# Hybrid encoder on one core: value halves stacked in one weight tile, key projections in another PSUM bank, four orders changed

## The reference, cut to what matters

```python
for l in range(2):                       # DEPTH = 2, 512 tokens, 1024 features
    h = rmsnorm(x, norm_mix_g[l])
    proj = h @ w_in[l]                   # latents for q (256), kv (128), k_pe (32), gate (1024)
    o_mla = mla_mixer(...)               # 8 heads; q = latent @ w_uq, [k | v] = latent @ w_ukv
    o_sg = spatial_gating_mixer(...)     # u * (W_s LayerNorm(v) + b), 4 chunks of 128 tokens, 8 groups
    x = x + concat([rmsnorm(o_mla), rmsnorm(o_sg)]) @ w_out[l]
    x = x + memory_attention(...)
    x = x + conv_ffn(...)
```

## Time and profile before

| what | value |
|---|---|
| median of 3 runs | 1485.91 us (1484.67 to 1487.13) |
| the profiled execution, its own time | 1485.62 us |
| its span | 1483.8 us |
| PE busy (matmuls) | 1455.2 us, 98% of the span |
| DVE / ACT / POOL busy | 734.9 / 698.3 / 683.9 us, 50 / 47 / 46% |
| mean granted TensorE clock | 0.996 of full speed |

### The profile page before, as it was taken

One profiled execution on the slowest core, in us unless ns is written; L12 is line 12 of the kernel. 1 busy time (PEld: TensorE's weight loads), 2 busy tenths in 40 slices (PEclk: granted clock), 3 DMA queues, 4 the chain that ended last, 5 costly groups with the idle time before them and its releaser, 6 DMA issues.

```text
span 1483.8 us, 19468 instructions
## 1 busy us (share of the span) xinstructions
PE 1455.2 (98%) x6872; PEld 1198.1 (81%) x6872; DVE 734.9 (50%) x1123; ACT 698.3 (47%) x1134; POOL 683.9 (46%) x343
## 2 busy tenths in 40 slices
PE   9999999999999999999999999999999999999997
PEld 7777789888888888888877777988888888888885
DVE  7738679353455410545264676771535544024533
ACT  6577656353344422444355885553534444224432
POOL 2445348534443454354445543684344354435351
PEclk9999999999999999999999999999999999999998
DMA  5320225412233333232323112463032332323231
GB/s 194 113 83 15 72 90 168 140 44 72 74 104 92 113 100 99 86 108 78 119 82 100 57 29 86 128 185 99 16 99 60 111 113 86 112 86 101 72 97 57
DMA packets 38889, 138.76 MB, mean 94 GB/s; under 512 B 4448, under 2 KB 4704, under 8 KB 38560
## 3 DMA queue, kind: packets, MB, share of 16 engines
q1 hardware_dynamic: 37296, 133.20, 29.2%
q10 hardware_dynamic: 1520, 4.56, 0.9%
HBM read 135.64 MB, written 2.10 MB: 93 GB/s over the span
## 4 chain that ended last, share of the span: by engine, by line
PE 78%; issue 9%; DVE 4%; POOL 4%; ACT 4%; DMA 0%; SPq 0%; POOLq 0%; DVEq 0%; ACTq 0%
PE ps L1461 25%; PE ps L1463 25%; PE ps L1462 25%; POOL w_lo L374 4%; PE ps L1619 1%; ACT work L660 1%; POOL work L442 1%; DVE small L1157 0%; DVE arena L1183 0%; DMA raw<-blocks_d 0%; DVE arena L1319 0%; ACT arena L668 0%; DVE work L1006 0%; ACT arena L633 0%; PE ps L1471 0%
## 5 line engine op out<-in xcount | busy, mean ns | idle before, releaser
L374 POOL TENSOR_TENSOR w_lo<-raw,w_hi 128x1024 fp32r<-128x1024 f32 x244 | 594.2, 2453 | 662.8 <-ACT w_hi L509 662.8
L509 ACT ACTIVATE w_hi<-raw 128x1024 fp32r<-128x1024 f32 x247 | 255.0, 1054 | 329.6 <-PE ps L1463 326.6
L1461 PE MATMUL ps<-h_hi,w_hi 128*128 128x512 f32 (+1 forms) x1040 | 406.8, 391 | 3.2 <-DVE w_lo L972 1.8
L1463 PE MATMUL ps<-h_hi,w_lo 128*128 128x512 f32 (+1 forms) x1040 | 403.7, 388 | 0.0
L1462 PE MATMUL ps<-h_lo,w_hi 128*128 128x512 f32 (+1 forms) x1040 | 403.6, 388 | 0.0
L1461 PE MATMUL ps<-arena,w_hi 128*128 128x512 f32 (+1 forms) x648 | 240.8, 372 | 0.0
L1463 PE MATMUL ps<-arena,w_lo 128*128 128x512 f32 (+1 forms) x648 | 238.8, 369 | 0.0
L1462 PE MATMUL ps<-arena,w_hi 128*128 128x512 f32 (+1 forms) x648 | 238.6, 368 | 0.0
L1461 PEld LDWEIGHTS ps<-h_hi,w_hi 128*128 128x128 f32 x1040 | 195.6, 188 | 46.8 <-issue 3.1
L1462 PEld LDWEIGHTS ps<-h_lo,w_hi 128*128 128x128 f32 x1040 | 195.7, 188 | 40.7 <-issue 1.0
L1463 PEld LDWEIGHTS ps<-h_hi,w_lo 128*128 128x128 f32 x1040 | 195.6, 188 | 40.6
(11 more groups left out here) (200 smaller groups left out, 1815.4 us busy)
## 6 DMA issues: line engine op xcount, KB each, us to landing
raw<-blocks_d SPq DMA_DIRECT2D x247, 512.0 KB, 3.5
work<-memT_d ACTq DMA_DIRECT2D x2, 1024.0 KB, 5.0
x<-xT_d SPq DMA_DIRECT2D x3, 512.0 KB, 7.5
work<-ln_d ACTq DMA_DIRECT2D x2, 512.0 KB, 3.7
outT_d<-work SPq DMA_DIRECT2D x4, 256.0 KB, 2.5
outT_d<-work ACTq DMA_DIRECT2D x4, 256.0 KB, 2.7
x<-xT_d SPq DMA_DIRECT2D x2, 256.0 KB, 4.6
raw<-blocks_d SPq DMA_DIRECT2D x2, 256.0 KB, 4.9
```

The lines of the kernel that those rows point to most:

```text
L374: gp.tensor_tensor(w_lo[:, b % SPLIT, :], raw[:, b % RAW, :], w_hi[:, b % SPLIT, :].bitcast(F32), ALU.subtract).then_inc(lo_done.sem, 1)
L509: act.activation(w_hi[:, b % SPLIT, :], raw[:, r, :], ACT.Copy).then_inc(hi_done.sem, 1)
L1461: pe.matmul(out, a_hi, b_hi, start=first, stop=False)
L1463: return pe.matmul(out, a_lo, b_hi, start=False, stop=last)
```

## The change

```diff
-NORM_STEPS = {(1, 2): 2, (2, 1): 3}
+CENTRED_STEPS = {(1, 1): 2, (1, 2): 3}
+NORM_STEP0 = (1, 2)
+NORM_STEPS = {(1, 3): 2, (2, 1): 3}
-SPLIT_STEPS = ((1, 3), (2, 3), (2, 3), (3, 0))
+SPLIT_STEPS = ((2, 0), (2, 3), (2, 3), (3, 0))
-MIX_STEPS = ((3, 2), (3, 3), (4, 2), (4, 3))
-GATED_STEPS = ((5, 0), (5, 2), (5, 2), (5, 3))
+MIX_STEPS = ((3, 2), (4, 1), (4, 3), (5, 1))
+GATED_STEPS = ((5, 2), (5, 2), (5, 3), (5, 3))
...
+        v_pair = arena[:, 8:16, :]...rearrange("p k (h s d) -> p k h s d", s=2, d=VD)
+        v_hi, v_lo = v_pair[:, :, :, 0, :], v_pair[:, :, :, 1, :]
...
         def k_bank(p):
-            return 5 if p == 0 else 2
+            return 5 if p == 0 else 4
+        def mix_bank(n):
+            return (4, 2)[n % 2]
... ACT
+                act.preload_act_table_set("gelu_apprx_tanh_and_others")   # ahead of the v_hi copies
...
-                def copy_sums(h):
-                    need(spread, h + 1)
+                def copy_part(h):
+                    need(pv_mm, h + 1)
                     if h > 0:
                         need(o_done, h)
-                    act.activation(rsum, ps[sum_bank(h)][0:64, :], ACT.Copy)
+                    act.activation(part, ps[B_PV][64:128, :], ACT.Copy)
+                    if t == 3 and h >= 1:
+                        copy_part(h - 1)
                     turned_hi(i)
-                    if t == 0 and h >= 1:
-                        copy_sums(h - 1)
-                    if t == 0 and h + 2 < HEADS:
+                    if t == h % 2 and h + 2 < HEADS:
                         q_part(h + 2)
-                    if h == HEADS - 1:
-                        gate_turned(t)
+                    if h == HEADS - 1 and t >= 1:
+                        gate_turned(t - 1)
... DVE
                 def attended(h):
-                    need(rsum_done, h + 1)
-                    need(pv_mm, h + 1)
-                    dve.tensor_tensor(o_mla[...], ps[B_PV][0:64, :], rsum, ALU.mult)
+                    need(part_done, h + 1)
+                    dve.tensor_tensor(part, ps[B_PV][0:64, :], part, ALU.add)
+                    need(whole_done, h + 1)
+                    need(spread, h + 1)
+                    dve.tensor_tensor(o_mla[...], ps[sum_bank(h)][0:64, :], part, ALU.mult)
-                    if t == 0 and h + 2 < HEADS:
+                    if t == h % 2 and h + 2 < HEADS:
                         q_part(h + 2)
+                    turned_lo(i)
                     if t == 3 and h >= 1:
                         attended(h - 1)
-                    turned_lo(i)
... PE
                 def q_proj(h):
                     if h >= 2:
                         need(qf_done, h)
+                        if h % 2 == 1:
+                            need(kl_done, h // 2 + 1); need(kst_done, h // 2 + 1)
+                        if h >= HEADS - 2:
+                            need(gated, 4 * (h - HEADS + 2) + 2)
                 def k_proj(p):
-                    if p > 1:
-                        need(rsum_done, 2 * p - 2)
+                    if p > 0:
+                        need(qf_done, 2 * p + 1)
                 def attend(h, ks):
                     for k in ks:
-                        last = product3(ps[B_PV][0:VD, :], v_hi[:, k, c], v_lo[:, k, c], pt_hi..., pt_lo...)
+                        pe.matmul(ps[B_PV][:, :], both, pt_hi[h % 2][:, k, :])      # both = [v_hi | v_lo]
+                        pe.matmul(ps[B_PV][0:VD, :], v_hi[:, k, h, :], pt_lo[h % 2][:, k, :])
                 def turn_gated(f):                    # f == 0: waits tile by tile for POOL
...                                                      # PE's loop
                         scores(i + 4)
+                    if t == 1 and h % 2 == 0 and h + 2 < HEADS:
+                        k_proj((h + 2) // 2)
                     turn(i)
-                    if t == 0 and h >= 1:
-                        spread_sums(h - 1)
                     if t in (1, 2) and h >= 1:
                         attend(h - 1, range(2 * t - 2, 2 * t))
-                    if t == 1 and h % 2 == 0 and h + 2 < HEADS:
-                        k_proj((h + 2) // 2)
-                    if t == 3 and h + 3 < HEADS:
+                    if t == 2 and h >= 1:
+                        spread_sums(h - 1)
+                    if t == 3 and h % 2 == 1 and h + 3 < HEADS:
                         q_proj(h + 3)
+                    if t == 0 and h % 2 == 1 and h + 2 < HEADS:
+                        q_proj(h + 2)
-                    if h == HEADS - 1:
-                        turn_gated(t)
+                    if h == HEADS - 1 and t >= 1:
+                        turn_gated(t - 1)
+                turn_gated(3)
```

More of the change, by code:

```diff
@@ L186, in encoder_program @@
         rs_tok, gsum = small[:, 60:64], small[:, 68:72]
-        rsum = work[0:64, 11, :]
+        part = work[0:64, 11, :]
         hsum, hrec = small[:, 80:88], small[:, 88:96]
@@ L632, in layer @@
                         block_used(B_WV)
[L633 removed]
+                    act.activation(v_hi[:, t], ps[BB[t]][:, :].rearrange("p (h d) -> p h d", d=VD), ACT.Copy)\
+                        .then_inc(vh_done.sem, 1)
                 for t in range(TT):
@@ L1627, in attend @@
                             need(o_done, h)
-                    c = slice(VD * h, VD * h + VD)
                     for k in ks:
-                        last = product3(ps[B_PV][0:VD, :], v_hi[:, k, c], v_lo[:, k, c],
-                                        pt_hi[h % 2][:, k, :], pt_lo[h % 2][:, k, :], k == 0, k == TT - 1)
+                        both = v_pair[:, k, h, :, :].rearrange("p s d -> p (s d)")
+                        if k < TT - 1:
+                            pe.matmul(ps[B_PV][:, :], both, pt_hi[h % 2][:, k, :], start=k == 0, stop=False)
+                        pe.matmul(ps[B_PV][0:VD, :], v_hi[:, k, h, :], pt_lo[h % 2][:, k, :], start=False, stop=False)
+                        if k == TT - 1:
+                            last = pe.matmul(ps[B_PV][:, :], both, pt_hi[h % 2][:, k, :], start=False, stop=True)
                     if ks[-1] == TT - 1:
@@ L1640, in spread_sums @@
                     elif h > 0:
-                        need(rsum_done, h)
-                    if h in (0, 2, 4):
-                        need(kl_done, h // 2 + 2)
-                        need(kst_done, h // 2 + 2)
-                    mixed_heads = 2 * sum(m < (h + 1, 0) for m in MIX_STEPS)
-                    if mixed_heads:
-                        need(gated, mixed_heads)
+                        need(o_done, h)
+                    if h in (3, 4):
+                        need(gated, 4 * (h - 2))
                     for t in range(TT):
@@ L1660, in mix @@
                         need(gated, 2 * n)
-                    need(rsum_done, MIX_STEPS[n][0])
-                    need(kl_done, MIX_STEPS[n][0] // 2 + 2)
-                    need(kst_done, MIX_STEPS[n][0] // 2 + 2)
+                    if n == 0:
+                        need(qf_done, 6)
+                    elif n == 2:
+                        need(kl_done, 4)
+                        need(kst_done, 4)
+                    else:
+                        need(o_done, MIX_STEPS[n][0] - 1)
                     wh, wl = halves(B_WS, P)
```

64 lines of the change are left out of this document (38 added, 26 removed).

## The result

The changed kernel takes **1498.26 us** (median of 4 runs, 1495.79 to 1500.09) where the kernel before takes 1485.76: a ratio of **1.0084, 95% interval 1.0072 to 1.0096**. It is slower by 12.5 us, outside the range of the prediction, which had 1484.3 and 1471 to 1490. The profiled execution is the fastest of the four, 1495.79 us, with a span of 1494.0 and a mean granted clock of 0.991; the other three ran at 0.987 to 0.989.

What follows compares the result with a forecast made beforehand. PE, 98% busy, was taken to set the whole, but ACT or DVE paces heads 0, 2 and 6. Terms −2.9 − 0.5 + 0.3 − 1.5 + 3.0 = −1.6 from 1485.6, plus 0.3 for the median: 1484.3 us, range 1471 to 1490.

Steps and rivals of the forecast that it cites:

- the attention loop's term: Attention loop, each layer: 12.3 us removed against 14.4 of new waits; taken as +1.5, twice, so +3.0.
- second rival: The clock falls in the wait at (2,1), costing 1.7 us per layer, 3.4 in all: 1487.7; chance 0.25.
- keys at (2,1): Head 2's keys, now ahead of `turn(9)`, wait for DVE's query scaling: 5.1 us where PE waited 2.1.
- query at (5,0): The query waits for the sixth `gated`, which DVE gives behind `attended(3)`: 1.8 us.
- `attend(5)` and `attend(6)`: In heads 5 to 7 these wait for `o_done`, behind the low part and a second DVE instruction: 1.3 and 1.0 us.
- `turn(29)`: In head 7 it waits 2.2 us for DVE's low part, a stretch formerly hidden behind POOL's wait.
- third rival: DVE's second instruction in `attended` shows in seven heads per layer: 10.1 us in all, about 1490; chance 0.15.
- The matmuls: `attend` drops from 12 to 8 per head; 64 matmuls at 0.23 us take 14.7 us off PE, 7.4 per layer.
- 1.9 for POOL: Head 7: gated tiles' transposes a step later, waiting tile by tile, remove 1.9 us of PE's wait per layer.
- The beginnings: Layer 0's start −2.9 us, latents −0.5 in layer 0 and +0.3 in layer 1, table for u −1.5.
- The first rival: PE stays the bound: all 14.7 us and the removed waits are gained, 1458, or 1471 with half the new waits; chance 0.2.
- The bounds: Attention loop per layer: −3 if 5.1 us of waits don't show, +4 if DVE's queue slips in four heads.

Runs made afterwards that it cites:

- e4: The changed kernel with 14 matmuls that nothing reads, filling PE's wait ahead of head 2's keys at (2,1): 1496.11 us, ratio 1.0071.
- e9: e1 with only the gated tiles' transposes in head 7 one step later, waiting tile by tile for POOL: 1485.11 us, ratio 0.9997.
- e7: The changed kernel without DVE's new instruction that adds the high part in `attended`: 1486.32 us, ratio 1.0001.
- e3: The changed kernel with twelve matmuls per head in `attend` again, the exponentials' low part counted twice: 1503.92 us, ratio 1.0117.
- e12: e10 with twelve matmuls per head in `attend` again, the low part's product counted twice: 1487.21 us, ratio 1.0004.
- e5: The changed kernel with tile 2's norm on DVE at (2,0) instead of (1,3), its split at (2,1): 1495.89 us, ratio 1.0067.
- e11: The changed kernel with head 7's gated transposes back in the scores' own step, tile by tile wait kept: 1495.2 us, ratio 1.0061.
- e10: The changed kernel with keys, tile 2's norm, gated heads at (4,3) and ACT's copy reordered, head 7's gated transposes back in their step: 1479.97 us, ratio 0.9955.
- e1: The kernel before with only the changed beginnings (layer 0's start, latents, table for u), attention loop untouched: 1483.13 us, ratio 0.9982.
- e6: The changed kernel with `gated_heads(2)` ahead of `attended(3)` on DVE at (4,3): 1491.39 us, ratio 1.0033.

## Why the prediction was wrong, point by point

**The step that failed** is the attention loop's term: "I take +1.5, twice: +3.0". It measured +6.4 and +6.7 in the profiled executions, beyond its own bound of +4 too. The sum priced PE's new waits as waits only and put the clock behind them at nothing. More than half of the miss is the clock. The prediction had seen it, as its second rival, and had left it out of the sum; and it had counted one place in each layer where there were two.

- *The waits.* In layer 0 PE's waits longer than 0.2 us inside the loop add up to 13.1 us (the seven shown, and five of 0.25 to 0.41), against 14.4 counted. By place: keys at (2,1) 5.1 forecast, 4.68 measured; query at (5,0) 1.8 and 2.23; `attend(5)` and `attend(6)` 1.3 and 1.0, measured 0.68 each; `turn(29)` 2.2 and 1.99, for DVE's low part as forecast; last gated transposes 0.8 and 0.69. The small ones of heads 0 to 4 came out smaller (`turn(4)` 1.0 and 0.28, keys at (4,1) 0.6 and 0.25), and one had no term: 0.67 at (3,3), ahead of `q_proj(6)`, for gated heads. The order of the queues, followed step by step, held. Up to `turn(12)` I had +0.45; measured from `turn(0)` it is +2.3, and +0.6 with the fall taken out.
- *The second rival, the clock.* It happened, at (2,1), in both layers, at the price given, 1.7 us each. But it also happened in head 7 in both layers, between waits of 1.99 and 0.68 us that I had priced as waits only. Four falls in the profile are 6.8 us, not 3.4 (at most: e4 and e9 show 1.5 and 1.6 for one). The other three runs have lower clocks still, and the median of the four lies 2.5 us above the profiled run, where I had put 0.3; that this is the clock rests on the mean clocks alone. These two are up to 9 us of the 14. The rule of the Trainium skill that stood beside this rival (TensorE: Matmul & The Clock Gate, "HAM oscillation — how this bites in real kernels") says that long waits between bursts throttle the engine again; the trace agrees for 4.7 us, and e4 shows the cause at (2,1), since filling the wait alone keeps the clock. For the falls in head 7 no run fills the wait, and the cause is argued from where they stand.
- *The third rival, DVE's second instruction.* I gave it 0.15 and a price of 5.5 us over the forecast. e7 takes 12.3 us away with it, 6.7 of waits and most of the rest clock. The mechanism was in part that of the rival, but not its place: `attend` waits only 0.7 four times; the instruction lengthens DVE's queue ahead of the waits that the change itself added, for `q_part` and the gated heads, and two of the four falls go with it.
- *What stays.* Without the falls the loop of layer 0 is 3.0 us longer, where the forecast had 1.5. The counted waits were 1.3 too many, so some 2.8 us a layer are lost beside them (2.2 if one goes by the sum's +2.1 and not by the +1.5 taken): part in first matmuls behind a wait (0.34 us to the next start at 108.98, where 0.23 is usual), part I can't place.
- *The matmuls.* 64 went, and a stacked product costs as much as a narrow one. But e3 prices them at 4.9 us in the changed loop and e12 at 7.3 in the mended one, and by the profiled executions they are worth about 8 in both. To take off 14.7 in full, as a first item of the balance, was right only as long as every wait behind it was counted too.
- *The norm at (1,3)* had its cost foreseen by the Trainium skill's rule (SBUF — State Buffer, "Who interferes with whom"), and the trace agrees: L1257, 1.81 us beside POOL's 1.72. The prediction named it and gave it no term in the sum. Against before its contention is 0.75 us more (1.06 there). e5 shows its whole 1.8 us in the keys' wait.
- *POOL's wait, "1.9 for POOL".* Taken as gone, against 2.2 and 0.8 of new waits; e9, with this part alone, has 0.9 a layer lost in waits, where these three terms say 1.1. Right, but booked as parts of a balance near nothing, its clock left out. e11 puts its undoing at 3.4 us, and e10, with the gate's squares moved too, at 5.6.
- *The beginnings.* The sum came at 25.98 (I had 25.5), the fall at the start went, the table gave 1.0 and 1.1 rather than 0.75 each. In the latents nothing was gained: PE waits 1.54 us ahead of the sums (the releaser isn't seen) where it waited 1.2. All three together are 2.7 us (e1), where the forecast had −2.9, −0.5, +0.3 and −1.5, 4.6; in e1's trace they are 4.0 by the start of layer 1's loop.
- *The first rival*, PE staying the bound, did not happen.
- *The bounds.* The 5.1 us "behind `attended` in heads 4 to 7", from which the lower bound comes, can't be added up from the terms given (1.8, 1.3 and 1.0 are 4.1). The outcome doesn't hang on it.

## What to carry to other kernels

On a tuned stream of matmuls a removed matmul is worth what the queues behind it allow; here a third by the medians in the loop as changed and half once the queues were put in order, and a little over half by the traces of both. So put new work on another engine only behind what the first engine waits for next, and count each longer wait of TensorE as a possible fall of its clock: in these kernels it came with some waits of 2 us and all of 4.3 or more, and cost about 1.6 us on top. Before a wait is removed, ask what else ran beneath it: the wait for POOL hid one for DVE's low part that was longer. And when a row names what a wait ended with, see whether that work was still needed: the row of `turn(29)` names ACT, whose part had been done for 4 us. An arrangement that loses can be a few reorderings from a gain: the same stacking lost 12.5 us and, with five small moves, won 6.7, 2.7 of them by the beginnings.

## What the runs showed of the hardware

- A fall of the granted clock lasted 3.4 us, at times 6.8, at half speed. With waits of 4.3 to 4.7 us at (2,1) it came each time (the change, e3, e6 and e11, both layers), within 0.6 us of the wait's end in six of the eight and 2 us ahead of it in two (layer 1 of e6 and e11). With 2.9 us there it came three times in four (e5 in both layers, e7 in layer 0 alone). With waits near 2 us it came sometimes: not in the kernel before or e1 at (2,1) (2.1 us), but in e9 at 114.1 with the same wait, in layer 0 and not in layer 1; and in head 7 of the change both times, of e9 never. So within one execution the same wait can have a fall in one layer and none in the other.
- The scatter of runs goes with it. Of the 17 runs of the kernel before beside e9, those with a mean clock of 0.997 took about 1484 us, the one with 0.993 took 1488.5: the runs of one kernel differ by how long they are at half clock. It matters then which execution a profile is of (the change's is its fastest, e6's its slowest: 3.0 us apart in the profiles, 7.6 in the medians).
- The reload of ACT's table took 1.28 us in its new place too, and there PE waits for nothing:
```profile
55.91 1.28 ACT L634 ACT_TABLE_LOAD   x1
```
